# Two chained transformer layers on one core: the second mixing input gets 1/rms at its evictions instead of in h

## What is computed

```python
def rms_norm(x, w):
    xf = x.astype(jnp.float32)
    y = xf * lax.rsqrt(jnp.mean(xf * xf, axis=-1, keepdims=True) + EPS)
    return (y * w.astype(jnp.float32)).astype(x.dtype)

# end of the first block
x = x + gate2 * rmsnorm(y, g_post_ffn[l])
# second block
h = rms_norm(x, norm_mix_w[i])
proj = h @ w_in[i]
q_a, k_a, v_a, q_g, k_g, v_g, r_g, gate_lr = split_cols(proj, IN_SPLITS)
# attention on q_a, k_a, v_a; gated linear attention (GLA) on the rest
gate_logit = gate_lr @ w_gla_gate_up[i] + b_gla_gate[i]
y_g = o_g * jax.nn.silu(r_g)
x = x + jnp.concatenate([y_a, y_g], axis=-1) @ w_out[i]
h = rms_norm(x, norm_ffn_w[i])
u = causal_depthwise_conv(h @ w_ffn_up[i], w_ffn_conv[i], b_ffn_conv[i])
u_gate, u_val = jnp.split(u, 2, axis=-1)
x = x + (jax.nn.gelu(u_gate) * u_val) @ w_ffn_down[i]
```

## Time and profile before

| What | Value |
|---|---|
| Three runs | 2810.56, 2810.79, 2812.27 us |
| Median | 2810.79 us |
| The profiled execution's own time | 2811.32 us |
| Its span | 2809.6 us |
| Mean granted clock of PE | 0.986 |
| PE busy | 2719.9 us, 97% |
| DVE, ACT, POOL busy | 64%, 46%, 10% |
| DMA, mean | 210 GB/s |

### The profile page before, as it was taken

How to read it: one execution, slowest core, us unless ns; L and a number is a source line. 1 busy time by engine, 2 the same in 40 slices (tenths; PEclk the granted TensorE clock), 3 DMA queues, 4 the chain that set the end, 5 groups by cost and what they waited for, 6 DMA issues and landing times.

```text
span 2809.6 us, 38901 instructions
## 1 busy us (share of the span) xinstructions
PE 2719.9 (97%) x14799; PEld 2340.4 (83%) x14799; DVE 1805.5 (64%) x2009; ACT 1295.8 (46%) x1556; POOL 292.1 (10%) x161
## 2 busy tenths in 40 slices
PE   4899999999899999999997999999999999999998
PEld 4798888788688888888886989878888888888887
DVE  7966779689965556655576444656666654666655
ACT  2256554334444444444444445535555533555454
POOL 2010121100000100001000000100113210131100
PEclk8899999999999999999998999999999999999999
DMA  9975646698945557755576554545555565555553
GB/s 373 349 261 191 223 150 225 226 325 310 322 140 190 193 198 251 254 180 191 182 254 229 166 171 144 165 139 180 186 189 179 179 209 183 192 180 190 184 197 133
DMA packets 299522, 588.70 MB, mean 210 GB/s; under 512 B 12282, under 2 KB 19438, under 8 KB 298510
## 3 DMA queue, kind: packets, MB, share of 16 engines
q1 hardware_dynamic: 292816, 577.84, 60.5%
q10 hardware_dynamic: 6590, 9.27, 1.0%
HBM read 584.98 MB, written 2.10 MB: 209 GB/s over the span
## 4 chain that ended last, share of the span: by engine, by line
PE 88%; DVE 7%; issue 2%; ACT 1%; DMA 1%; SPq 0%; POOL 0%; DVEq 0%; POOLq 0%; ACTq 0%
PE psum L780 13%; PE psum L784 13%; PE psum L782 13%; PE bank L973 12%; PE psum L973 12%; PE bank L976 6%; PE psum L976 6%; PE psum L791 2%; PE psum L795 2%; PE psum L793 2%; DVE ada_acc L864 2%; DVE mod_acc L651 2%; DVE w_lo L738 2%; PE bank L946 1%; PE bank L2594 1%
## 5 line engine op out<-in xcount | busy, mean ns | idle before, releaser
L738 DVE TENSOR_TENSOR w_lo<-raw,w_hi 128x1024 fp32r<-128x1024 f32 x912 | 1157.0, 1286 | 835.9 <-ACT w_hi L726 826.0
L726 ACT ACTIVATE w_hi<-raw 128x1024 fp32r<-128x1024 f32 x912 | 953.1, 1054 | 1260.9 <-PE psum L784 580.7
L973 PE MATMUL psum<-h_both,w_hi 128*128 128x512 f32 x1408 | 496.5, 397 | 0.8 <-DVE x L2362 0.7
L973 PE MATMUL bank<-h_both,w_hi 128*128 128x512 f32 x1408 | 495.3, 396 | 0.0
L976 PE MATMUL bank<-h_both,w_lo 128*128 128x256 f32 x1408 | 395.0, 281 | 0.0
L976 PE MATMUL psum<-h_both,w_lo 128*128 128x256 f32 x1408 | 394.9, 280 | 0.0
L780 PE MATMUL psum<-w_hi,h_both 128*128 128x512 f32 x880 | 348.4, 396 | 1.3 <-ACT tokbuf L1810 0.7
L784 PE MATMUL psum<-w_hi,h_both 128*128 128x512 f32 x880 | 343.5, 390 | 0.0
L782 PE MATMUL psum<-w_lo,h_both 128*128 128x512 f32 x880 | 343.4, 390 | 0.0
L973 PEld LDWEIGHTS psum<-h_both,w_hi 128*128 128x128 f32 x1408 | 264.2, 188 | 64.1 <-DVE x L2362 1.0
L973 PEld LDWEIGHTS bank<-h_both,w_hi 128*128 128x128 f32 x1408 | 264.1, 188 | 63.3
(11 more groups left out here) (361 smaller groups left out, 3172.8 us busy)
## 6 DMA issues: line engine op xcount, KB each, us to landing
raw<-in_w_in_dram SPq DMA_DIRECT2D x120, 1024.0 KB, 5.1
raw<-in_w_ffn_in_dram SPq DMA_DIRECT2D x88, 1024.0 KB, 5.0
raw<-in_w_ffn_up_dram SPq DMA_DIRECT2D x88, 1024.0 KB, 5.1
raw<-in_w_ada_dram SPq DMA_DIRECT2D x64, 1024.0 KB, 5.2
raw<-in_w_ffn_out_dram SPq DMA_DIRECT2D x44, 1024.0 KB, 5.1
raw<-in_w_ffn_down_dram SPq DMA_DIRECT2D x44, 1024.0 KB, 5.1
ada_raw<-in_w_ada_dram SPq DMA_DIRECT2D x64, 512.0 KB, 8.0
raw<-in_w_out_dram SPq DMA_DIRECT2D x32, 1024.0 KB, 5.2
```

The source lines that it names most:

```text
L726: nc.scalar.activation(w_hi[:, slot, :, 0:ncol], raw[:, rs, 2 * h:2 * h + 2, 0:ncol], ACT.Copy).then_inc(split_hi, inc)
L738: nc.vector.tensor_tensor(w_lo[:, slot, :, 0:ncol], raw[:, rs, 2 * h:2 * h + 2, 0:ncol], w_hi[:, slot, :, 0:ncol].bitcast(F32), ALU.subtra ...
L973: pe.matmul(region[:, f, :].rearrange("p (s t) -> p s t", s=2), w_hi[:, slot, kk, cols_], h_both[:, :, k, :], start=first, stop=False, ski ...
```

## The change

In the second mixing input x is transposed without 1/rms, block of columns by block of columns as the residual makes them, and only the gain enters h. ACT's squares are spread between its h_hi splits. 1/rms enters behind the products: as a per-partition scale of two ACT operations where tokens are on partitions (v, the output gate, v of the GLA), and as a factor along the free axis where tokens are there. For the latter PE multiplies an all-ones matrix by diag after group 0, which gives 1/rms of all 256 tokens on every partition (`r_row`); DVE copies it to SBUF and evicts groups 0 to 3, 6 and 7 and gate_lr with it, instead of ACT. DVE's split of half 3 moves from ahead of the residual to the fifth tile, and ACT's load of w_up_g into group 1. In the second feed-forward the split of the fifth half of the value group goes ahead of the gate group's taps, on ACT and on DVE.

```diff
+        r_row = sb("r_row", [P, TOK])
...
+        def residual_columns_dve(dve, r, c):
+
+            for t in range(TT):
+                part = slice(c * COLS, (c + 1) * COLS)
+                nc.vector.scalar_tensor_tensor(x[:, t, part], tokbuf[:, t, part], stats[:, r, 2 + t:3 + t],
+                                               x[:, t, part], ALU.mult, ALU.add
+                                               ).then_inc(sem("x_ready"), 1)
+
+        def residual_square_act(act, r, c, t):
+
+            act.wait_ge(sem("x_ready"), 8 * (r // 2) + 2 * c + t + 1)
+            nc.scalar.activation(junk[:, t * COLS:(t + 1) * COLS], x[:, t, c * COLS:(c + 1) * COLS], ACT.Square,
+                                 accum_out=part_sq[:, 1, t, c:c + 1]).then_inc(sem(f"part_squares{r + 1}"), 1)
+            act.wait_ge(sem(f"part_squares{r + 1}"), TT * c + t + 1)
...
-            residual_squares_act(act, 3)
+            for c in range(D // COLS):
+                residual_square_act(act, 3, c, 0)
+                for b in (2 * c, 2 * c + 1):
+                    if b > 4:
+                        split_w_hi(act, plan.mix_in2, 0, b - 1, b)
+                    gained_pair_act(act, "norm2", b, gain_of("norm_mix_w_2"))
+                residual_square_act(act, 3, c, 1)
+            split_w_hi(act, plan.mix_in2, 0, 7, 8)
...
-            split_act(act, "norm2", h_hi, KD, gain_of("norm_mix_w_2"), between=plan.mix_in2)
...
-                    if at == (4, 1):
-                        act.wait_ge(bank_full[1], filled("low_rank", 1))
-                        nc.scalar.activation(gate_lr[:], bank[0:RANK, 1, 0:TOK], ACT.Copy).then_inc(bank_free[1], 1)
-                    if g <= 12 and s == 2:
+                    if g in (4, 5, 9, 10, 11, 12) and s == 2:
                         act.wait_ge(w_used, ph.done(0, g))
                         ps, free = psum[ph.pair[g]], psum_free[ph.pair[g]]
-                        flat = ps[:].rearrange("p b (f t) -> p (b f) t", t=TOK)
-                        if g < 2:
-                            nc.scalar.activation(q2_t[:, 4 * g:4 * g + 4, :], flat, ACT.Copy,
-                                                 scale=HD ** -0.5).then_inc(free, 1)
...
+                        if g < 6:
+                            dst, kind = va[:, :, (g - 4) * COLS:(g - 3) * COLS], ACT.Copy
                         elif g < 11:
-                            nc.scalar.activation(
-                                tokbuf[:, :, D // 2 + (g - 9) * COLS:D // 2 + (g - 8) * COLS],
-                                ps[:], ACT.Silu).then_inc(free, 1)
+                            dst = tokbuf[:, :, D // 2 + (g - 9) * COLS:D // 2 + (g - 8) * COLS]
+                            kind = ACT.Silu
...
+                            dst, kind = vg[:, :, (g - 11) * COLS:(g - 10) * COLS], ACT.Copy
+                        for t in range(TT):
+                            ins = nc.scalar.activation(dst[:, t, :], ps[:, t, :], kind,
+                                                       scale=stats[:, 4, 2 + t:3 + t])
+                        ins.then_inc(free, 1)
...
+                        if g == 0:
+                            split_w_hi(act, ph, i, *span(ph, 1, part=(0, 1)))
...
-                            split_w_hi(act, ph, i, *span(ph, 1, part=(0, 2)))
+                            split_w_hi(act, ph, i, *span(ph, 1, part=(1, 2)))
...
-            split_w_lo(dve, plan.mix_in2, 0, 3, 4)
             dve.wait_ge(sem("y_gated"), 4)
-            residual_dve(dve, chain, 3)
-            normed_dve(dve, 4)
-            split_dve(dve, "norm2", h_hi, h_lo, KD, gain_of("norm_mix_w_2"), between=plan.mix_in2)
+            dve.wait_ge(sem("rms"), 4)
+            residual_columns_dve(dve, 3, 0)
+            residual_columns_dve(dve, 3, 1)
+            for b in range(KD // 2):
+                if b >= 4:
+                    split_w_lo(dve, plan.mix_in2, 0, b - 1, b)
+                gained_pair_dve(dve, "norm2", b, gain_of("norm_mix_w_2"))
+                if b < 2:
+                    residual_columns_dve(dve, 3, 2 + b)
+            split_w_lo(dve, plan.mix_in2, 0, 7, 8)
+            part_sums_dve(dve, 4, part_sq[:, 1])
 
             ph = plan.mix_in2
             for g in range(len(ph.groups)):
                 for s, part in enumerate(parts(ph, g)):
                     at = g, s
-                    split_w_lo(dve, ph, 0, *span(ph, g, part=part if g else ((4, 8), (8, 8), (8, 8))[s]))
+                    if at == (0, 0):
+                        split_w_lo(dve, ph, 0, *span(ph, 0, part=(4, 6)))
+                        normed_dve(dve, 4)
+                        split_w_lo(dve, ph, 0, *span(ph, 0, part=(6, 8)))
+                    elif g:
+                        split_w_lo(dve, ph, 0, *span(ph, g, part=part if at != (7, 2) else (6, 7)))
+                    if at == (0, 2):
+                        dve.wait_ge(bank_full[0], filled("r_row", 0))
+                        nc.vector.tensor_copy(r_row[:], bank[:, 0, 0:TOK]).then_inc(bank_free[0], 1)
+                        dve.wait_ge(bank_free[0], emptied("r_row", 0))
+                    if at == (4, 1):
+                        dve.wait_ge(bank_full[1], filled("low_rank", 1))
+                        nc.vector.tensor_tensor(gate_lr[:], bank[0:RANK, 1, 0:TOK], r_row[0:RANK, :], ALU.mult
+                                                ).then_inc(bank_free[1], 1)
+                    if g in (0, 1, 2, 3, 6, 7) and s == 2:
+                        dve.wait_ge(w_used, ph.done(0, g))
+                        flat = psum[ph.pair[g]][:].rearrange("p b (f t) -> p (b f) t", t=TOK)
+                        per_token = r_row[:].unsqueeze(1).to_broadcast([P, 4, TOK])
+                        if g < 2:
+                            ins = nc.vector.scalar_tensor_tensor(q2_t[:, 4 * g:4 * g + 4, :], flat, HD ** -0.5,
+                                                                 per_token, ALU.mult, ALU.mult)
+                        else:
+                            dst = k2_t[:, 4 * (g - 2):4 * (g - 1), :] if g < 4 else (qg if g == 6 else kg)[:]
+                            ins = nc.vector.tensor_tensor(dst, flat, per_token, ALU.mult)
+                        ins.then_inc(psum_free[ph.pair[g]], 1)
+                    if at == (7, 2):
+                        split_w_lo(dve, ph, 0, *span(ph, 7, part=(7, 8)))
...
-                        split_w_lo(dve, ph, i, *span(ph, g, part=(begun, 8) if g == 0 else None))
+                        split_w_lo(dve, ph, i, *span(ph, g, part=(1 if g else begun, 8)))
...
+                        if g == 0:
+                            split_w_lo(dve, ph, i, *span(ph, 1, part=(0, 1)))
...
+            ph = plan.mix_in2
+            for b in range(4):
+                pe.wait_ge(sem("x_ready"), 8 + 2 * (b // 2 + 1))
+                transpose_pair_pe(pe, "norm2", x, b)
+            for h in range(KD // 2):
+                products(pe, ph, 0, 0, h_hi, h_lo, transposed=True, ready="norm2", part=(h, h + 1))
+                if h < 4:
+                    pe.wait_ge(sem("x_ready"), 8 + 2 * (h // 2 + 3))
+                    transpose_pair_pe(pe, "norm2", x, 4 + h)
             pe.wait_ge(sem("normed"), 6)
-
-            ph = plan.mix_in2
-            normed_products(pe, ph, "norm2", 4, transposed=True)
+            pe.wait_ge(bank_free[0], fill("r_row", 0))
+            for t in range(TT):
+                mm = pe.matmul(bank[:, 0, t * P:(t + 1) * P], ones[:], diag[:, t, :], start=t == 0,
+                               stop=t == TT - 1, skip_group_check=True)
+            mm.then_inc(bank_full[0], 1)
```

More of the change, by code:

```diff
@@ L345, in bank_uses @@
         ("up1_1", (FFN_PARTS[1][1],) * 4), ("mod_down1", (0, 0, 0, 2)),
-        ("norm2", (2, 2, 2, 2))]
+        ("norm2", (2, 2, 2, 2)), ("r_row", (1, 0, 0, 0))]
     for at in sorted(SIDE_2):
@@ L1730, in _ @@
                           ).then_inc(sem("toep_full"), 16)
-            split_act(act, "norm2", h_hi, KD, gain_of("norm_mix_w_2"), between=plan.mix_in2)
-            act.wait_ge(sem("rms"), 5)
-            act.dma_start(w_up_g[:], a["w_gla_gate_up_2"][0]).then_inc(sem("w_up_g_full"), 16)
             ph = plan.mix_in2
@@ L1740, in _ @@
                     split_w_hi(act, ph, 0, *span(ph, g, part=part if g else ((4, 8), (8, 8), (8, 8))[s]))
+                    if at == (1, 0):
+                        act.wait_ge(sem("rms"), 5)
+                        act.dma_start(w_up_g[:], a["w_gla_gate_up_2"][0]).then_inc(sem("w_up_g_full"), 16)
                     if at == (10, 0):
@@ L1765, in _ @@
                         ps, free = psum[ph.pair[g]], psum_free[ph.pair[g]]
-                        flat = ps[:].rearrange("p b (f t) -> p (b f) t", t=TOK)
-                        if g < 2:
-                            nc.scalar.activation(q2_t[:, 4 * g:4 * g + 4, :], flat, ACT.Copy,
-                                                 scale=HD ** -0.5).then_inc(free, 1)
-                        elif g < 4:
```

(19 more changed lines are left out.)

## The result

The changed kernel takes 2795.95 us, median of 4 runs (2792.23 to 2796.57); the kernel before, in the same comparison, 2811.53 (2810.56 to 2813.8). The ratio is 0.9941, 95% interval 0.9923 to 0.9958: some 15.6 us faster, where 10.85 was forecast. The profiled execution took 2796.57 us, its span is 2794.8; against the profiled execution of before (2811.32) that is 14.75 us.

A forecast was written before the change was run, and what follows sets the result against it. PE, busy 97% of the span, was taken as the bound, leaving its idle stretches, removable work and low clock. 10.05 + 1.6 - 0.8 - 0.5 + 0.5 = 10.85 us off 2811.32 gave 2800.5 us, range 2798.6 to 2804.4.

The forecast's parts named there:

- Part 1: Turn from feed-forward to second mixing input: transposing x without 1/rms, by column blocks, brings the first product 10.05 us earlier.
- Part 2: Group 0 of the second mixing input: identity transposes between products are cheaper, 4 x 0.4 = 1.6 us saved.
- Part 3: PE's clock after the turn: full 3.4 to 5.05 us after restart, so the first products lose 0.8 us.
- The first rival: Identity transposes don't warm PE's clock, which counts from the first product: 2.8 us lost instead of 0.8, 2802.5 us; chance 0.33.
- The warning of the earlier trace: At 304 us PE was busy yet fell to half clock at 305.3: light work can count for too little.
- Part 4: Behind group 0: PE's ones times diag for the r row adds 0.5 us; diag in time by 1.2 us.
- The second rival: diag comes late for the r row, so PE stands 1.6 us behind group 0: 2802.1 us; chance 0.10.
- Part 5: Evictions moved from ACT to DVE lie beside PE; earlier kg ahead of group 9 saves 0.5 us.
- The half ahead of the softmax: Half 60, split by DVE ahead of a softmax: a delay of 2.4 us from the added evictions would fit.
- Part 6: Second feed-forward: splitting the value group's fifth half (half unit) ahead of the taps brings 0, at most 11 x 0.1 us either way.
- Nothing comes of it: At the turn PE still idles 7.2 us and the wait moves to the tiles: 2811.3 us; chance 0.04.
- slower: PE's clock stays at half through group 0 because light transposes count too little: 2822.7 us; chance 0.03.

The follow-up runs named there:

- e9: The kernel before, unchanged, run again for a second profile: 2810.58 us, ratio 1.0004.
- e1: The kernel before with only the fifth half of the value group split ahead of the taps: 2803.68 us, ratio 0.9999.
- e5: The changed kernel itself, run again in the third session: 2795.63 us, ratio 0.9955 to the kernel before.
- e11: The changed kernel itself, run again in the fourth session for a third profile: 2793.42 us, ratio 0.9948.
- e3: The changed kernel with the fifth half split late, as before, in one iteration only, the second of the first part: 2793.58 us, ratio 0.9962.
- e6: The changed kernel with the fifth half split behind the taps again, in the third session on another chip: 2794.27 us, ratio 0.9955.
- e2: The changed kernel with the fifth half split behind the taps, as before, second session: 2795.17 us, ratio 0.9962.
- e4: The changed kernel with the 32 transposes of x done as products with the plain identity: 2796.57 us, ratio 0.9969.
- e8: The changed kernel with only the columns undone, all eight pieces of x made and squared before the first tile: 2798.62 us, ratio 0.9968.
- e10: The changed kernel with DVE evicting kg behind both weight splits, not between them: 2798.62 us, ratio 0.9961.
- e7: The changed kernel with each up-projection tile row's four 512-column matmuls first, then the four of 256 columns: 2796.7 us, ratio 0.9962.

## Why the prediction was right, and where it was not

**Freed of the pace.** A microsecond at the slower pace does the work of 347/353.3 of one at the faster, so it loses 0.0178. Taken off the profiled times, before gives 2811.32 - 648 x 0.0178 = 2799.8, e9 2799.0 and e1 2799.5, mean 2799.4; after gives 2796.57 - 458 x 0.0178 = 2788.4, e5 2787.1, e11 2787.9, e3 2788.3, e6 2788.2 and e2 2786.1, mean 2787.7. Of these nine, e1 is the kernel before and e2, e3 and e6 are the changed kernel but for the place of the half unit. By them the change is worth 11.7 us, against 10.85 forecast.

**Part 1** was right in its chain and short by a term. From DVE's first piece to PE's restart are 1.47 us (forecast 1.46), from there to the first product 3.39 (3.42): cold transposes against the identity are 0.21 us apart, the upper of the two bounds. Gained were 11.0 us instead of 10.05, and the odd 0.9 lies ahead of all that: POOL's first operation takes 0.19 us in every kernel with the new turn and 1.09 to 1.10 in before, e1 and e9, though its instruction is the same. "All is as before up to DVE's start" was the step that failed by this much. In the kernel before, DVE splits a half just then:

```profile
1521.37 1.22 DVE L738 TENSOR_TENSOR w_lo<-raw,w_hi 128x1024 fp32r<-128x1024 f32 x1
1521.54 1.09 POOL L1111 TENSOR_SCALAR stats<-stats 128x2 f32<-128x2 f32 x1 [105.36 <-DVE stats L1137]
```

In all three profiles with the old turn POOL's operation begins during this split and ends 0.05 us behind it, so it looks as if the split held it up. The change moved the split away, which was counted for DVE and not for POOL. No run moves that split alone.

**Part 2.** A half with a pair behind it takes 3.31 us, forecast 3.37, and took 3.77: 1.84 saved for 1.6.

**Part 3.** The clock came back 1.40 us behind the first product, and products issued 0.21 us apart until then instead of 0.12, about 0.7 lost (0.8 forecast). The earlier trace rows show less, 16 matmuls against 24, since the second of its windows isn't 256-column products throughout: from 140.6 us on it holds 512-column ones. The first rival needed at least 3.4 us. Over seven further profiles with identity transposes, columns interleaved, it came 3.7 to 4.9 us after the restart, that is 0.3 to 1.5 after the first product; so the mechanism was right, and that this profile lost almost what was forecast is luck. The rule of the Trainium skill (TensorE: Matmul & The Clock Gate, Part 4: PE-mode transpose), that the full clock doesn't engage for transpose-mode matmuls, is thus not borne out here: by it the clock would have stayed at half for 3.4 us of products or more. Nor do products show an advantage: with the identity the clock came back 3.28 us after the restart (e4), with diag after 5.07 (before), 4.51 (e1) and 3.05 (e9). In the first layer's turn, where all thirteen profiles have the same 32 records with diag, it came 2.8 to 6.1 us after the restart, more than the 3.4 to 5.05 that the forecast took from two readings. The warning of the earlier trace rows is an event of some executions too: the clock falls near 305 us in before, e1, e6, e8 and e10 and not in the other eight, e9 among them, which is the same program as before.

**Part 4.** The r row costs 0.37 us (0.5 forecast), with no wait:

```profile
1554.12 0.61 PE L2767 MATMUL bank<-diag,ones 128*128 128x128 f32 x4
1554.49 0.36 PE L792 MATMUL psum<-h_both,w_hi 128*128 128x256 f32 x1
```

diag is there by 1551.3, 2.8 us ahead; the margin forecast was 1.2. The second rival is out. Parts 2 to 4 together: from the first product to the convolution's transposes 66.21 us instead of 66.99, 0.78 saved where 0.3 was summed.

**Part 5.** From the scores to group 9 PE takes 0.57 us less (0.5 forecast), with nothing waited for; e10 shows that the place in DVE's program decides it, by 2 us. The half ahead of the softmax stopped nobody. DVE is busy 11.7 us more, 7 were forecast, all of it beside PE.

**Sum of the turn.** 11.0 + 0.78 + 0.57 = 12.35 us. The yardstick repeats it: 425.3 to 425.8 us in after, e2, e3, e5, e6 and e11, against 437.8 in before, 437.9 in e1 and 436.8 in e9, whose clock was back 2 us sooner. In this pair of profiles 1.2 of it is taken back ahead of the change, since the changed kernel ended its feed-forward at 1518.62 instead of 1517.40, in code that is the same: 0.4 had gathered by the first layer's turn, and there the full clock came back at 779.14 us instead of 776.35, which makes the other 0.8. So 11.1 is the difference at 1956 us.

**Part 6** is the step that put the forecast outside its range: without its 3.7 us the profiled execution would have taken 2800.3. It was priced at 0, at most 11 x 0.1 us, from the waits of PE. That view can't show what moved: PE waits for nothing, its matmuls come closer. In this pair of profiles that gave 3.7 us more. Whether the half unit did it stays open: the faster pace followed in this part wherever the half unit was in, but it isn't needed for it (e6), and it moved no median where it was tried alone (e1 0.9999; e5 and e6 the same ratio). The part's own sign, no change, stood; what failed is that the sum and the range held no term for the pace. Its price goes from 4.2 us (236 x 0.0178) to 11.5 (648 x 0.0178) over the profiles, and from 4.2 to 8.8 among those of the changed kernel itself. The text named the sign of it, a changed period of the up-projection, but gave it no price and no chance.

**The other rivals.** *Nothing comes of it* and *slower* are out: no tile past the first stops PE, and the clock holds through group 0.

## What to carry over

A factor that scales whole rows can leave the operand and enter at the product's eviction; then the work in front of the first product is no longer the norm but the first block of columns, and the chain should be cut into such blocks on every engine, or a good part of the gain goes into a new wait (e8). A step moved beside a stream of matmuls that waits for nothing can still be followed by a change of the stream's own spacing: compare the starts of a periodic operation over whole stages, and put the spread of the same kernel between executions and chips into the range. Where an effect of 0.1% is argued from two profiles, repeat both kernels before believing it.

## What the hardware did that I had not expected

- A stream that alternates 512- and 256-column matmuls without any wait at full clock has two paces, 347 and 353 ns a pair, and can change from one to the other in the middle of a group. With equal sizes next to each other (e7) there is one, 350 to 352 ns.
- The same two-column POOL operation took 0.19 us in this turn when no DVE operation ran at its start, and 1.09 to 1.10 us in the three profiles in which it began during one of DVE's weight splits; it then ended 0.05 us behind the split.
- A wait of 1.99 us behind small score products (e10) was followed by 3.4 us at half clock; a wait of 0.50 us at the same place (before, e1, e9) was not.
- When PE stood idle 3.82 us behind its transposes (e8), the clock came only 11.5 us after the restart and 4.0 us after the first product, though 16 transposes had run.
